# Odd attention: value products in 256-column pairs, grouped by branch

## The chip, the cores and the metric

The kernel runs on one core of a Trainium2 chip, in one launch. The metric is the device time of that core in microseconds, the median of several runs. All matrix products named here are in float32.

## The reference

Two small networks run one after the other on 512 tokens of width 1024. The second one has two layers; the change lies in its second layer, called odd, which is an attention with 16 heads of 64 in four groups that share keys and values, and three branches. Cut to what matters here:

```python
def nsa_attention(q, kc, vc, ks, vs, kw, vw, gate_logit, ...):
    # compressed branch: one key for each stride of 16 tokens (31 of them)
    p_cmp = masked_softmax(q @ k_cmp.T * scale - slopes * distance, cmp_end <= t)
    # selected branch: with 8 blocks and topk = 8 every block is selected
    p_slc = masked_softmax(q @ ks.T * scale - slopes * distance, key <= t)
    # window branch: 512 tokens, here all earlier tokens
    p_win = masked_softmax(q @ kw.T * scale - slopes * distance, key <= t)
    return g0 * (p_cmp @ v_cmp) + g1 * (p_slc @ vs) + g2 * (p_win @ vw)

def odd_layer(x, ...):
    o = nsa_attention(...)
    return x + (o * silu(z)) @ w_out
```

## The kernel before, in words

One instruction stream for each engine is written out by hand, with semaphores between them. The stage that matters is the odd attention: ahead of it stand the projections of the odd layer, behind it the output projection (`oout`, lines 720 to 722 for its products) and the last normalisation.

The 16 heads are taken as eight pairs t = 0..7; both heads of a pair (e = 0, 1) use the same keys and values, those of group g = t // 2. The 512 tokens are four tiles a = 0..3 of 128, and tile a sees the key tiles b = 0..a. Two branches with full keys (`ks`, `vs` and `kw`, `vw`) give ten products of weights by values for each head and branch. They are cut into five parts u, so that each part fills a bank of 512 columns: `ODD_TILES` lists, for each part, (branch, tile a, first column):

- u=0: branch 0, a=3 (one tile of 512 columns)
- u=1: branch 0, a=2 and a=0 (384 and 128)
- u=2: branch 1, a=3
- u=3: branch 1, a=2 and a=0
- u=4: a=1 of branch 0 and of branch 1 (256 and 256)

In the code branch 0 is the selected branch (`ks`, `vs`) and branch 1 the window (`kw`, `vw`). The compressed branch is a part of its own, "blocks", one for each group, so in the list `ODD` it stands in every even pair between u=1 and u=2. `ODD` has 44 parts.

A part n goes through these steps:

1. TensorE, `odd_scores` (L1273; for blocks L1267): scores into one of two PSUM banks PS.
2. VectorE, `odd_x` (L2418): adds the distance table, takes the negative maximum, writes `od_x` (four places). For blocks L2401 to L2410.
3. ScalarE, `odd_exp` (L1737; blocks L1731): exponentials and their sums.
4. VectorE, `odd_invert` (L2440; blocks L2429, L2431): reciprocal of the sums.
5. GpSimd (L2650; blocks L2638, L2641): multiplies by the reciprocal and the gate. It also makes the distance tables (L2629), and low parts of some weights (L2499).
6. TensorE, `odd_transposes` (L1293; blocks L1285): eight 128 x 128 transposes into PC, four for each head. It waits for the copies of the part before.
7. VectorE copies head 0's half of PC (L2457), ScalarE head 1's half (L1754), into `od["PT"]`, which has two places, used in turn; blocks have one copy, by VectorE (L2461).
8. TensorE, `odd_outputs` (L1319): the value products into PD, bank t % 2. The values of one key tile are the stationary operand (64 columns, for head e at partitions 64 e), the transposed weights the moving one, 128 columns each: four products for each head in each part. Blocks have `block_outputs` (L1299, L1302), two products of 512 columns, one for each of the group's two pairs.

After u=4, VectorE multiplies PD by the gate z (L2469, semaphore `ny_raw`), ScalarE copies the result to its rounded part (L1776) and VectorE takes the rest (L2473).

TensorE's order in step n is: transposes of part n, scores of part n+3, outputs of part n-1. VectorE's is: copy of n, `odd_x` of n+3, the reciprocal of n+2, and what follows a pair. ScalarE's is: copy of n, exponentials of n+3, the rounded copy after a pair, and in eight of the steps a piece of the output projection's weights (L1745).

Of the kernel before, what the change touches and what calls it, by code (L numbers as in the profile page):

```python
# [15 lines left out]
ACT = mybir.ActivationFunctionType  # L16
# [3 lines left out]
P = 128  # L20
# [3 lines left out]
S = 512  # L24
# [21 lines left out]
DH = 64  # L46
# [96 lines left out]
for _step in SSD:  # L143
# [5 lines left out]
    if _what in ("B", "C", "x", "z", "s"):  # L149
# [41 lines left out]
ODD = [part for t in range(NH // 2)  # L191
       for part in [("pair", t, 0), ("pair", t, 1)] + ([("blocks", t // 2, 0)] if t % 2 == 0 else []) +
       [("pair", t, u) for u in range(2, 5)]]
# [31 lines left out]
def build(nc, x_in, stream, down, params_in, tables_in, out):  # L225
    ctx = ExitStack()
    with ctx:
# [16 lines left out]
        def sem(name):  # L244
            if name not in sems:
                sems[name] = ctx.enter_context(nc.semaphore(name))
            return sems[name]
# [16 lines left out]
        PC = ctx.enter_context(nc.psum_tensor("PC", [P, 2, BANK], F32))  # L264
        PD = ctx.enter_context(nc.psum_tensor("PD", [P, 2, BANK], F32))
# [5 lines left out]
        def carve(fields):  # L271

            at, views = 0, {}
            for name, *dims in fields:
                n = int(np.prod(dims))
                v = arena[:, at:at + n]
                if len(dims) == 2:
                    v = v.rearrange("p (a b) -> p a b", a=dims[0])
                elif len(dims) == 3:
                    v = v.rearrange("p (a b c) -> p a b c", a=dims[0], b=dims[1])  # L280
                elif len(dims) == 4:
                    v = v.rearrange("p (a b c d) -> p a b c d", a=dims[0], b=dims[1], c=dims[2])
                views[name] = v
                at += n
            assert at <= ARENA, at
            return views
# [129 lines left out]
        def slot_of(stage, r):  # L416
            return nth_plain(stage, r) % R
# [5 lines left out]
        def tile_of(stage, j):  # L423
            return PS[(M0[stage] + j) % 2]
# [96 lines left out]
        def mix_s(n, e):  # L521
            return PS[n % 2][:, e * BANK:(e + 1) * BANK]

        od = carve([("q", 8, S), ("z", 8, S), ("A2", 2, NG, 16, CB + 2), ("ksd", NG, S), ("kwd", NG, S), ("vs", 4, 256), ("vw", 4, 256),
                    ("gates", 48, 4), ("cmp_bias", NH, P), ("h1", 2, P), ("h1v", 2, NG, 4, CB), ("kcmp", P),
                    ("hb", 4), ("mxc", 16), ("rsc", 16), ("cfc", 16), ("cg", NH, 4), ("nm", 4, 4), ("rs", 4, 4),
                    ("gap", 60), ("Vbd", NG, 256), ("PT", 2, 2, S), ("PTc", S)])
# [11 lines left out]
        uT_flat = uT[:, :, :].rearrange("p k l -> p (k l)")  # L539
# [5 lines left out]
        def odd_before(n):  # L545

            pairs = sum(kind == "pair" for kind, _, _ in ODD[:n])
            return pairs, n - pairs

        def odd_tiles(n):  # L550

            return [(b, a, at, P * (a + 1)) for b, a, at in ODD_TILES[ODD[n][2]]]
# [138 lines left out]
        def _(pe):  # L691
            mm = nc.tensor.matmul
# [61 lines left out]
            def project_units(stage, units, moving, high=None, ready=None, within=None):  # L754

                first = units[0] if isinstance(units, range) else 0
                for r in units if isinstance(units, range) else range(units):
                    unit_ready(stage, 0, r)
                    for m in range(2):
                        acquire(pe, stage, 0, 2 * R, 2 * r + m)  # L760
                        new = r == first and m == 0
                        project(stage, 0, 2 * R, 2 * r + m, r, KD, m * P, moving, high, ready if new else None,
                                within if new else None).then_inc(ps_full, 1)
# [450 lines left out]
            for a in range(4):  # L1214
                for k in range(KD):
                    last = mm(tile_of("od_g", 0)[:, a * 48:(a + 1) * 48], h2[:, k, a * P:(a + 1) * P], w_g[:, k, :],
                              start=k == 0, stop=k == KD - 1)
# [8 lines left out]
            for which, stage in enumerate(("ck", "cv")):  # L1226
                for hid in range(2):
                    unit_ready(stage, 0, hid)
                    acquire(pe, stage, 0, 2, hid)
                    t = tile_of(stage, hid)  # L1230
                    w = ring[:, slot_of(stage, hid), :].rearrange("p (k m) -> p k m", k=16)
                    for l2 in range(16):
                        last = mm(t[:, 0:NG * CW].rearrange("p (g c) -> p g c", g=NG), w[:, l2, :],
                                  od["A2"][:, which, :, 2 * l2 % 16, l2 // 8:l2 // 8 + CW], start=l2 == 0, stop=l2 == 15)
# [61 lines left out]
            def block_outputs(g):  # L1296

                pe.wait_ge(sem("cpt_full"), g + 1)
                mm(PD[:, 0, :], od["Vbd"][:, g, 0:P], od["PTc"], start=False, stop=True, skip_group_check=True)  # L1299
                if g:  # L1300
                    pe.wait_ge(sem("ny_raw"), 2 * g)
                mm(PD[:, 1, :], od["Vbd"][:, g, P:2 * P], od["PTc"], start=True, stop=True)  # L1302

            def odd_outputs(n):

                _, t, u = ODD[n]
                f, _ = odd_before(n)
                g = t // 2
                if n == 0:
                    pe.wait_ge(sem("od_full"), 5)  # L1310
                    pe.wait_ge(sem("zs_full"), 16)
                if u == 0 and t % 2 == 0 and t:
                    pe.wait_ge(sem("ny_raw"), t - 1)
                pe.wait_ge(sem("ns_c0"), f + 1)
                pe.wait_ge(sem("ns_c1"), f + 1)
                for branch, a, at, w in odd_tiles(n):
                    for b in range(a + 1):
                        for e in range(2):
                            last = mm(PD[DH * e:DH * e + DH, t % 2, a * P:(a + 1) * P],  # L1319
                                      od["vw" if branch else "vs"][:, b, g * DH:(g + 1) * DH],  # L1320
                                      od["PT"][:, f % 2, e, at + b * P:at + (b + 1) * P],
                                      start=u == 0 and t % 2 == 0 and b == 0, stop=True,
                                      skip_group_check=True)
                if u == 4:
                    last.then_inc(sem("no_full"), 1)

            unit_ready("od_z", 0, 3)
            late_gate(0)
# [9 lines left out]
            for n in range(len(ODD) + 1):  # L1338
                if n < len(ODD):
                    odd_transposes(n)  # L1340
                if n + 3 < len(ODD):
                    odd_scores(n + 3)
                if n and ODD[n - 1][0] == "pair":
                    odd_outputs(n - 1)
                elif n:
                    block_outputs(ODD[n - 1][1])
            project_units("oout", 4, yl, yh, (sem("y_full"), 8))
            stats("last", S)

# [2 lines left out]
        def _(act):  # L1352
            A = nc.scalar.activation
# [315 lines left out]
            for n in range(len(MIX) + 4):  # L1669
                t = n // 7  # L1670
# [28 lines left out]
            for which, stage in enumerate(("ck", "cv")):  # L1699
                for hid in range(2):  # L1700
                    tile_wait(act, stage, 0, 2, hid)
                    t = tile_of(stage, hid)
# [46 lines left out]
            def odd_copy(n):  # L1749
                f, c = odd_before(n)  # L1750
                if ODD[n][0] == "blocks":
                    return
                act.wait_ge(sem("ns_t"), 2 * f + 2)
                A(od["PT"][:, f % 2, 1, :], PC[:, 1, :], ACT.Copy).then_inc(sem("ns_c1"), 1)  # L1754

            for n in range(2):
                odd_exp(n)
# [10 lines left out]
            for n in range(len(ODD) + 3):  # L1768
# [4 lines left out]
                if n >= 3 and ODD[n - 3][0] == "pair" and ODD[n - 3][2] == 4:  # L1773
                    t = ODD[n - 3][1]
# [9 lines left out]
        def _(dve):  # L1784
            V = nc.vector
# [535 lines left out]
            for n in range(len(MIX) + 5):  # L2321
                t = n // 7
# [130 lines left out]
            for n in range(len(ODD) + 4):  # L2453
                if n < len(ODD) and ODD[n][0] == "pair":
                    f, _ = odd_before(n)
                    dve.wait_ge(sem("ns_t"), 2 * f + 1)
                    V.tensor_copy(od["PT"][:, f % 2, 0, :], PC[:, 0, :]).then_inc(sem("ns_c0"), 1)  # L2457
                elif n < len(ODD):
                    _, c = odd_before(n)
                    dve.wait_ge(sem("ct_full"), c + 1)  # L2460
                    V.tensor_copy(od["PTc"], PC[:, 0, :]).then_inc(sem("cpt_full"), 1)  # L2461
                if n + 3 < len(ODD):
                    odd_x(n + 3)
                odd_sum(n + 2)
                odd_invert(n + 2)
                if n >= 2 and n - 2 < len(ODD) and ODD[n - 2][0] == "pair" and ODD[n - 2][2] == 4:
                    t = ODD[n - 2][1]
                    dve.wait_ge(sem("no_full"), t + 1)
                    V.tensor_tensor(sq[:, t % 2, 0:S], PD[:, t % 2, :], od["z"][:, t, :], ALU.mult).then_inc(sem("ny_raw"), 1)  # L2469
                if n >= 4 and n - 4 < len(ODD) and ODD[n - 4][0] == "pair" and ODD[n - 4][2] == 4:  # L2470
                    t = ODD[n - 4][1]
                    dve.wait_ge(sem("ny_high"), t + 1)
                    V.tensor_tensor(r32(yl[:, t, :], 0), sq[:, t % 2, 0:S], split(yh[:, t, :], 0), ALU.subtract  # L2473
                                    ).then_inc(sem("y_full"), 1)
# [318 lines left out]
```

## Time and profile before

| | us |
|---|---|
| median of 3 runs | 2307.72 |
| lowest and highest run | 2302.77, 2310.04 |
| the profiled execution, its own time | 2307.89 |
| span of its profile | 2306.1 |
| odd attention in it, about | 2095.3 to 2248.0 |

The profiler gives each instruction's engine, line, start and duration. A float32 product is run in two passes, so it stands as two instructions (a group of eight value products, four for each head, is x16). The timelines merge neighbouring instructions of one line: the first number is the start, the second the time from the first start to the last end, in square brackets stands the idle time before and what ended it. "issue" is a wait that the profile puts down to no one. Ends of products are modelled, so the distances between starts are the safer measure.

### The profile page before, as it was taken

Reading aid. Unit: us, or ns where it says so; the run is one execution under the profiler, and the core shown is the slowest. Engines: PE = TensorE matmul, PEld = TensorE weight load, DVE = VectorE, ACT = ScalarE, POOL = GpSimd, SP = SyncE. Lnnn points to the kernel's source line nnn. Section 1 sums busy time; section 2 is a strip of 40 time slices with the busy share of each in tenths; the row PEclk is TensorE's granted clock in tenths of the full one; section 3 lists DMA queues with packets and bytes.
Section 4 is the critical chain, followed back from the end, with each engine's and each line's share of the span. In section 5 each row is a group of like instructions: output and inputs, shape, how many; then the busy total and the mean of one; then the engine's idle time right before and its main releaser. Section 6 shows DMA issues by size and latency. Waiting matters only on the chain.

```text
span 2306.1 us, 38488 instructions
## 1 busy us (share of the span) xinstructions
PE 2212.1 (96%) x15924; PEld 1935.8 (84%) x15924; DVE 1240.1 (54%) x1874; ACT 905.4 (39%) x1447; POOL 1006.1 (44%) x924
## 2 busy tenths in 40 slices
PE   8999999889999999999998999999999999999997
PEld 7898988889999999985698989987786577886666
DVE  6776777868527734344369716743214641115763
ACT  4564645533223233346433312333113532126762
POOL 4445444565555540032246555544344234334751
PEclk9999999999999999999999999999999999999999
DMA  4211122122222222220022222222222012350000
GB/s 164 77 72 66 64 74 74 37 74 92 76 99 92 75 100 97 87 74 1 1 92 74 75 102 102 85 77 92 92 92 100 28 56 90 99 179 38 24 15 37
DMA packets 29372, 175.59 MB, mean 76 GB/s; under 512 B 3984, under 2 KB 4496, under 8 KB 12304
## 3 DMA queue, kind: packets, MB, share of 16 engines
q1 hardware_dynamic: 29200, 173.14, 21.3%
q8 instruction: 126, 2.06, 0.4%
q14 instruction: 46, 0.38, 0.0%
HBM read 166.71 MB, written 2.10 MB: 73 GB/s over the span
## 4 chain that ended last, share of the span: by engine, by line
PE 77%; DVE 9%; issue 4%; ACT 3%; POOL 3%; DVEq 2%; SPq 1%; DMA 0%; ACTq 0%; POOLq 0%
PE PS L720 19%; PE PS L721 19%; PE PS L722 19%; POOL ring_r L2490 2%; DVE arena L1933 2%; PE PS L1029 2%; PE PS L1273 2%; PE PC L1293 2%; PE PD L1319 2%; PE PD L720 1%; PE PD L721 1%; PE PD L722 1%; DVE arena L2151 1%; PE PD L1059 1%; DVEq L408 1%
## 5 line engine op out<-in xcount | busy, mean ns | idle before, releaser
L722 PE MATMUL PS<-arena_r,ring_r 128*128 128x264 f32 (+2 forms) x3520 | 1076.9, 306 | 0.0
L2490 POOL TENSOR_TENSOR ring_r<-ring,arena_r 128x512 fp32r<-128x512 f32 (+1 forms) x456 | 596.4, 1338 | 803.6 <-ACT arena_r L1410 803.6
L722 PEld LDWEIGHTS PS<-arena_r,ring_r 128*128 128x128 f32 x3520 | 667.5, 190 | 30.1
L720 PE MATMUL PS<-arena_r,arena_r 128*128 128x264 f32 (+2 forms) x2160 | 654.1, 303 | 17.0 <-POOL arena_r L2508 6.2
L721 PE MATMUL PS<-arena_r,arena_r 128*128 128x264 f32 (+2 forms) x2160 | 647.6, 300 | 0.0
L720 PE MATMUL PS<-arena_r 128*128 128x264 f32 (+3 forms) x1552 | 488.1, 315 | 11.7 <-POOL ring_r L2490 5.1
L1410 ACT ACTIVATE arena_r<-ring 128x2048 fp32r<-128x2048 f32 (+1 forms) x144 | 258.5, 1795 | 499.8 <-PE PS L722 452.6
L720 PEld LDWEIGHTS PS<-arena_r,arena_r 128*128 128x128 f32 x2160 | 409.1, 189 | 41.2 <-issue 9.8
L721 PE MATMUL PS<-uT_r,arena_r 128*128 128x264 f32 (+2 forms) x1360 | 429.9, 316 | 0.0
L721 PEld LDWEIGHTS PS<-arena_r,arena_r 128*128 128x128 f32 x2160 | 409.7, 190 | 13.2 <-issue 0.5
L720 PEld LDWEIGHTS PS<-arena_r 128*128 128x128 f32 x1552 | 295.0, 190 | 33.5 <-POOL ring_r L2490 6.0
L721 PEld LDWEIGHTS PS<-uT_r,arena_r 128*128 128x128 f32 x1360 | 259.2, 191 | 16.8 <-issue 0.5
L2499 POOL TENSOR_TENSOR ring_r<-ring,arena_r 128x512 fp32r<-128x512 f32 x128 | 181.7, 1446 | 160.3 <-ACT arena_r L1410 159.5
L2091 DVE TENSOR_TENSOR hT<-hT,PS 128x512 f32<-128x512 f32 (+2 forms) x56 | 38.8, 693 | 239.7 <-PE PS L722 239.4
L2151 DVE SCALAR_TENSOR_TENSOR arena<-arena,par 128x528 f32<-128x528 f32 (+1 forms) x176 | 158.9, 903 | 13.1
L1539 ACT ACTIVATE arena<-PS 128x528 f32<-128x528 f32 (+1 forms) x76 | 46.0, 605 | 252.3 <-PE PS L722 252.0
L1839 DVE TENSOR_TENSOR arena<-PS,sd 128x512 f32<-128x512 f32 (+1 forms) x46 | 32.0, 697 | 171.6 <-PE PS L722 171.1
L2148 DVE TENSOR_SCALAR arena<-arena,par 128x528 f32<-128x528 f32 (+1 forms) x88 | 79.1, 899 | 67.6 <-ACTq L408 63.6
L2650 POOL TENSOR_SCALAR arena<-arena 128x128 f32<-128x128 f32 (+3 forms) x128 | 78.7, 627 | 68.4 <-DVE arena L2440 68.1
L722 PE MATMUL PD<-arena_r,ring_r 128*128 128x264 f32 (+1 forms) x336 | 97.3, 289 | 0.0
L1933 DVE SCALAR_TENSOR_TENSOR arena<-arena,par 128x528 f32<-128x528 f32 x72 | 79.3, 1101 | 5.9 <-issue 0.5
L1737 ACT ACTIVATE arena<-arena 128x128 f32<-128x128 f32 (+3 forms) x128 | 71.1, 556 | 27.5 <-DVEq L408 22.8
(389 smaller groups left out, 3038.9 us busy)
## 6 DMA issues: line engine op xcount, KB each, us to landing
ring<-stream SPq DMA_DIRECT2D x130, 1024.0 KB, 4.8
ring<-down SPq DMA_DIRECT2D x32, 704.0 KB, 4.0
hT<-x_in SPq DMA_DIRECT2D x4, 528.0 KB, 7.6
arena<-tables SPq DMA_DIRECT2D x4, 512.0 KB, 3.8
arena<-arena SPq DMA_DIRECT2D x16, 128.0 KB, 2.4
out<-uT SPq DMA_DIRECT2D x4, 512.0 KB, 2.8
par<-params SPq DMA_DIRECT2D x1, 1634.5 KB, 14.1
arena<-arena SPq DMA_DIRECT2D x8, 136.0 KB, 3.5
```

Of the source, the lines that this page charges most:

```text
L720: mm(out_, r32(ah), r32(bh), start=start, stop=False)
L721: mm(out_, r32(ah), r32(b), start=False, stop=False)
L722: return mm(out_, r32(a), r32(bh), start=False, stop=stop)
L1029: return mm(sb_z(u, e)[:, a:a + rhs.shape[1]], w, rhs, start=False, stop=True, skip_group_check=True)
L1410: A(r32(high_slot(h)[:, 0:width]), raw_slot(h)[:, 0:width], ACT.Copy).then_inc(sem("high_full"), 1)
L1737: A(x, x, ACT.Exp, bias=od["nm"][:, n % 4, i:i + 1], scale=-1.0, accum_out=od["rs"][:, n % 4, i:i + 1])
L1933: last = V.scalar_tensor_tensor(cv, raw[:, k:k + L], w(k), cv, ALU.mult, ALU.add)
L2148: V.tensor_scalar(out_, ffn[raw][:, 0:width], w(0), b, ALU.mult, ALU.add)
L2151: last = V.scalar_tensor_tensor(out_, ffn[raw][:, k:k + width], w(k), out_, ALU.mult, ALU.add)
L2490: last = G.tensor_tensor(r32(low[:, cut]), raw[:, cut], split(high[:, cut]), ALU.subtract)
L2499: last = G.tensor_tensor(r32(low[:, cut]), raw[:, cut], split(high[:, cut]), ALU.subtract)
L2650: last = G.tensor_scalar(x, x, od["rs"][:, n % 4, i:i + 1], od["gates"][:, 6 * t + 3 * e + 1 + b, a:a + 1], ALU.mult, ALU.mult)
```

## The change

The value products are put in another order and in wider pieces. After the transposes of u=0 and u=1 nothing is multiplied; their copies go to two places of a branch, and the products of the branch follow later: in the step of u=2 those of key tiles 0 and 1, in the step of u=3 those of key tiles 2 and 3. The products of branch 1 (parts u=2 and u=3) all stand in the step of u=4. Part u=4 itself is multiplied in the step after it, as before (`odd_second`). Where a key tile b has weights for both tiles 2 and 3, the two are the moving operand of one product, 256 columns from two places (`pair[:, :, e, ...]`), into 256 neighbouring columns of PD. There are four places for weights: two of branch 0 in `od["PT"]`, two of branch 1 in the second half of uT. `block_outputs` now begins both banks of PD (start=True), with its wait on `ny_raw` written for each, and all products of the two other branches add to what stands there.

```diff
+        def odd_weights(branch):
+            return od["PT"] if branch == 0 else uT_flat[:, 4 * S:8 * S].rearrange("p (n e c) -> p n e c", n=2, e=2)
+        def odd_slot(n):
+            u = ODD[n][2]
+            return odd_weights(u in (2, 3))[:, int(u in (0, 2)), :, :]
...
             def block_outputs(g):
                 pe.wait_ge(sem("cpt_full"), g + 1)
-                mm(PD[:, 0, :], od["Vbd"][:, g, 0:P], od["PTc"], start=False, stop=True, skip_group_check=True)
-                if g:
-                    pe.wait_ge(sem("ny_raw"), 2 * g)
-                mm(PD[:, 1, :], od["Vbd"][:, g, P:2 * P], od["PTc"], start=True, stop=True)
-
-            def odd_outputs(n):
+                for half in range(2):
+                    if 2 * g + half > 1:
+                        pe.wait_ge(sem("ny_raw"), 2 * g + half - 1)
+                    elif half == 0:
+                        pe.wait_ge(sem("od_full"), 5)
+                        pe.wait_ge(sem("zs_full"), 16)
+                    mm(PD[:, half, :], od["Vbd"][:, g, half * P:(half + 1) * P], od["PTc"], start=True, stop=True)
+
+            def odd_values(t, e, branch, b, a, weights):
+                n = weights.free_size() // P
+                return mm(PD[DH * e:DH * e + DH, t % 2, a * P:(a + n) * P], od["vw" if branch else "vs"][:, b, t // 2 * DH:(t // 2 + 1) * DH],
+                          weights, start=False, stop=True, skip_group_check=True)
+
+            def odd_branch(n, blocks):
                 _, t, u = ODD[n]
+                branch = u // 2
                 f, _ = odd_before(n)
-                g = t // 2
-                if n == 0:
-                    pe.wait_ge(sem("od_full"), 5)
-                    pe.wait_ge(sem("zs_full"), 16)
-                if u == 0 and t % 2 == 0 and t:
-                    pe.wait_ge(sem("ny_raw"), t - 1)
+                pe.wait_ge(sem("ns_c0"), f + 1)
+                pe.wait_ge(sem("ns_c1"), f + 1)
+                pair = odd_weights(branch)
+                for b in blocks:
+                    for e in range(2):
+                        if b < 3:
+                            odd_values(t, e, branch, b, 2, pair[:, :, e, b * P:(b + 1) * P])
+                        else:
+                            odd_values(t, e, branch, b, 3, pair[:, 1, e, b * P:(b + 1) * P])
+                    if b == 0:
+                        for e in range(2):
+                            odd_values(t, e, branch, 0, 0, pair[:, 0, e, 3 * P:4 * P])
+
+            def odd_second(n):
+                _, t, _ = ODD[n]
+                f, _ = odd_before(n)
                 pe.wait_ge(sem("ns_c0"), f + 1)
                 pe.wait_ge(sem("ns_c1"), f + 1)
                 for branch, a, at, w in odd_tiles(n):
-                    for b in range(a + 1):
+                    for b in range(2):
                         for e in range(2):
-                            last = mm(PD[DH * e:DH * e + DH, t % 2, a * P:(a + 1) * P],
-                                      od["vw" if branch else "vs"][:, b, g * DH:(g + 1) * DH],
-                                      od["PT"][:, f % 2, e, at + b * P:at + (b + 1) * P],
-                                      start=u == 0 and t % 2 == 0 and b == 0, stop=True,
-                                      skip_group_check=True)
-                if u == 4:
-                    last.then_inc(sem("no_full"), 1)
+                            last = odd_values(t, e, branch, b, a, odd_slot(n)[:, e, at + b * P:at + (b + 1) * P])
+                last.then_inc(sem("no_full"), 1)
+
+            def odd_outputs(n):
+                kind, t, u = ODD[n - 1]
+                if kind == "blocks":
+                    block_outputs(t)
+                elif u == 4:
+                    odd_second(n - 1)
+                if n < len(ODD):
+                    kind, t, u = ODD[n]
+                    if kind == "pair" and u in (2, 3):
+                        odd_branch(n - u + 1 - (t % 2 == 0), range(2) if u == 2 else range(2, 4))
+                    elif kind == "pair" and u == 4:
+                        odd_branch(n - 1, range(4))
...
-                if n and ODD[n - 1][0] == "pair":
-                    odd_outputs(n - 1)
-                elif n:
-                    block_outputs(ODD[n - 1][1])
+                if n:
+                    odd_outputs(n)
...
-                A(od["PT"][:, f % 2, 1, :], PC[:, 1, :], ACT.Copy).then_inc(sem("ns_c1"), 1)
+                A(odd_slot(n)[:, 1, :], PC[:, 1, :], ACT.Copy).then_inc(sem("ns_c1"), 1)
...
-                    V.tensor_copy(od["PT"][:, f % 2, 0, :], PC[:, 0, :]).then_inc(sem("ns_c0"), 1)
+                    V.tensor_copy(odd_slot(n)[:, 0, :], PC[:, 0, :]).then_inc(sem("ns_c0"), 1)
```

## Rows read from the trace of the kernel before

**Rows 1.** The page, part 1: busy time and share of the span, instructions.

```profile
PE 2212.1 (96%) x15924; PEld 1935.8 (84%) x15924; DVE 1240.1 (54%) x1874; ACT 905.4 (39%) x1447; POOL 1006.1 (44%) x924
```

**Rows 2.** Stages: window, length, busy of PE, PEld, DVE, ACT, POOL; granted clock; DMA.

```profile
2095.30:2248.00 152.70, 140.94 (x1338) 100.60 (x1337) 109.21 (x362) 110.78 (x308) 99.52 (x151) 0.99 0.05 15
2133.10:2136.50 3.40, 3.40 (x27) 3.02 (x26) 2.42 (x5) 1.39 (x3) 1.35 (x3) 0.50 0.00 0
```

**Rows 3.** Timeline of TensorE, pair t=5 from u=0, then pair t=6.

```profile
2195.16 1.06 PE L1293 MATMUL PC<-par,arena 128*128 128x128 f32 x8 [0.53 <-issue]
...
2197.22 1.09 PE L1319 MATMUL PD<-arena 128*64 128x128 f32 x16
...
2199.27 1.14 PE L1273 MATMUL PS<-arena 64*128 64x256 f32 x8
...
2201.95 1.06 PE L1293 MATMUL PC<-par,arena 128*128 128x128 f32 x8 [0.53 <-issue]
2202.95 1.13 PE L1273 MATMUL PS<-arena 64*128 64x512 f32 x4
...
2208.54 1.07 PE L1293 MATMUL PC<-par,arena 128*128 128x128 f32 x8 [0.32 <-issue]
2209.54 1.98 PE L1267 MATMUL PS<-arena 64*128 64x32 f32 x32
...
2212.47 1.09 PE L1293 MATMUL PC<-par,arena 128*128 128x128 f32 x8
2213.49 1.13 PE L1273 MATMUL PS<-arena 64*128 64x512 f32 x4
...
2217.86 1.09 PE L1319 MATMUL PD<-arena 128*64 128x128 f32 x16
2218.89 0.66 PE L1285 MATMUL PC<-par,arena 128*128 128x128 f32 x4
2219.47 1.14 PE L1273 MATMUL PS<-arena 64*128 64x256 f32 x8
...
2232.74 1.06 PE L1293 MATMUL PC<-par,arena 128*128 128x128 f32 x8 [0.53 <-issue]
```

**Rows 4.** Timelines of VectorE (first row) and ScalarE, same pair t=5.

```profile
2197.34 0.56 DVE L2418 CUSTOM_DVE_ANT_0 arena<-PS,uT 128x384 f32<-128x384 f32 x1 [0.82 <-PE PS L1273]
...
2198.87 0.61 ACT L1737 ACTIVATE arena<-arena 128x384 f32<-128x384 f32 x1 [1.41 <-DVEq L408]
...
2201.26 0.60 ACT L1754 ACTIVATE arena<-PC 128x512 f32<-128x512 f32 x1
...
2207.33 0.63 ACT L1776 ACTIVATE arena_r<-sq 128x512 fp32r<-128x512 f32 x1
2207.87 0.58 ACT L1754 ACTIVATE arena<-PC 128x512 f32<-128x512 f32 x1
```

**Rows 5.** Timeline of TensorE, the stage's end: two groups of value products together.

```profile
2245.69 1.97 PE L1319 MATMUL PD<-arena 128*64 128x128 f32 x32
2247.59 0.50 PE L720 MATMUL PS<-arena_r,arena_r 128*128 128x512 f32 x1
```

**Rows 6.** Timelines of GpSimd and VectorE, the blocks of pair t=6.

```profile
2217.55 1.05 POOL L2641 TENSOR_TENSOR arena<-arena 128x512 f32<-128x512 f32 x1
...
2220.23 0.68 DVE L2461 COPY arena<-PC 128x512 f32<-128x512 f32 x1
```

**Rows 7.** The chain that ended last, pair t=6: start, length, what.

```profile
2223.72 1.05 PE PD L1299 x2
...
2225.63 0.32 issue
```

**Rows 8.** Timeline of TensorE around the drop of the clock, end of pair t=1.

```profile
2130.27 1.07 PE L1293 MATMUL PC<-par,arena 128*128 128x128 f32 x8 [0.84 <-issue]
...
2133.18 1.97 PE L1319 MATMUL PD<-arena 128*64 128x128 f32 x16
2135.09 1.76 PE L1293 MATMUL PC<-par,arena 128*128 128x128 f32 x8
```

## The prediction

> **What bounds the kernel now.** I read the page's first part first: TensorE is busy for 96% of the span [rows 1], so a change matters only through TensorE's time or through its waits. Next the table by stages: the odd attention takes about 152.7 us, and TensorE is busy for 140.94 of them [rows 2]. So about 12 us of waiting are open in this stage. In the timeline of TensorE I then looked at what precedes each start. A step n is three groups: the transposes of part n, the scores of part n+3, the value products of part n-1. From one start to the next the transposes take 1.00 to 1.02 us, the scores 1.06 (both together 2.06, from 2195.16 to 2197.22), the products 1.03 (2217.86 to 2218.89), so a full step is 3.1 us; some steps have 0.3 to 0.5 us of idle time before their transposes [rows 3].
>
> That idle time has one cause. ScalarE copies part n's second half out of PSUM, then does the exponentials of part n+3, then copies part n+1; TensorE may not transpose part n+2 before this last copy. In an odd pair: the scores end, the product group behind them starts at 2197.22; VectorE takes the scores from 2197.34, ScalarE's exponentials run from 2198.87, its copy from 2201.26 for 0.60, the transposes start at 2201.95 [rows 3, 4]. So from E, the end of the score group, to the transposes two steps on, the **chain** is 4.73 us. TensorE's own way over the same distance (products, transposes, scores, products) is 1.03 + 2.07 + 1.03 = 4.13, which is why it idles. For parts of one 512-column tile the chain is shorter: from E = 2202.95 + 1.06 = 2204.01 to 2208.54 it is 4.53, and of this 0.54 is the copy L1776 that stands between (2207.33 to 2207.87) [rows 3, 4]; 3.99 without it.
>
> **The change, part by part.**
>
> *Wider products.* The columns that stream stay the same: of a branch, tile a=3 has four products, a=2 three and a=0 one; three of these eight now go along with another, so five products of 256, 256, 256, 128 and 128 columns have the same 1024. What a wider product saves is shown by the scores: four instructions of 512 columns take 1.13 us, eight of 256 columns 1.14 [rows 3]. Columns set the time, the number of instructions does not. I take 0 to 0.01 us per branch, at most 0.2 us for 16 branches, and count it as nothing.
>
> The Trainium skill, TensorE: Matmul & The Clock Gate, Back-to-back issue gap, speaks otherwise: in streams of weight load and matmul it has about 81 ns per matmul at 128 columns and 131 at 512, so that four times the columns cost only 1.6 times as much. An estimate by that page would put a 256-column product near 98 ns where two narrow ones take 162. The trace doesn't agree: 1.13 against 1.14 us at equal columns. What the rule would do here is the second rival below.
>
> *Moved products.* A unit is one 128-column product for both heads, four instructions in the trace. Two value groups back to back, 32 instructions, take 2247.59 - 2245.69 = 1.90 us, one of 16 takes 1.03 [rows 3, 5]; so a unit costs 0.2175 us and a group 0.16 us beside. Before, each step has four units: 1.03. After, in the order of the steps: u=0 four (the second part, as before), u=1 none, blocks none, u=2 five (1.25), u=3 three (0.81), u=4 eight (1.90). A pair has 20 units as before, and one or two groups fewer.
>
> *Waits.* The two copies that a branch waits for are those that the step's own transposes have waited for already; nothing new is queued behind them. The block products keep their place, and their second half waits for the same reading of PD. The four weight places add no wait: each is overwritten by a copy behind a transpose that TensorE issues after the last product that reads it. The copies keep their size and engine, no DMA moves, nothing on SP or GpSimd changes.
>
> *An odd pair, both kernels*, T = start of the transposes, 0 at u=0, E = T + 2.07:
> - u=1: 2.07 + 1.03 = 3.10 in both.
> - u=2: before TensorE would be ready at 6.20, after at 5.17; the chain from E = 2.07 ends at 6.80 in both. The time won is idle.
> - u=3: before 6.80 + 3.10 = 9.90; after 6.80 + 2.07 + 1.25 = 10.12.
> - u=4: TensorE 13.00 in both, chain 6.80 + 2.07 + 4.53 = 13.40 in both.
> - next u=0, past the block scores, which take 1.90 instead of 1.06 (2209.54 to 2212.47, less 1.03): before 13.40 + 1.00 + 1.90 + 1.03 = 17.33 (the trace has 2212.47 - 2195.16 = 17.31), after 13.40 + 2.90 + 1.90 = **18.20**. That is **+0.87**.
>
> So units are taken from a step that waits for ScalarE in any case and given to one, u=4, where TensorE is last.
>
> *An even pair, after*, 0 at u=0. u=1: 3.10. Blocks: TensorE 5.17, but GpSimd's product L2641 ends 2217.55 + 1.05 - 2214.55 = 4.05 after E (2213.49 + 1.06), with 0.15 to react 6.27 (before 6.42). u=2: TensorE 7.91; VectorE's copy L2461 ends at 2220.91, 3.05 after E of u=1 (2217.86), with 0.1 to react 3.10 + 2.07 + 3.15 = 8.32 (before 2219.47 + 1.07 + 1.03 - 2212.47 = 9.10, since TensorE still had a group there). u=3: 8.32 + 2.07 + 1.91 for the block products (2223.72 to 2225.63) + 1.25 = 13.55 (before 13.48, of which the last 0.32 was a wait). u=4: + 2.88 = 16.43. Next u=0: + 2.07 + 1.90 = **20.40**, against 2232.74 - 2212.47 = 20.27 before: **+0.13** [rows 3, 6, 7]. Here 0.78 us are won up to u=2 and lost again in u=2 and u=4.
>
> *Sum.* Four odd pairs at 0.87 and about three and a half even ones at 0.13: 3.5 + 0.5 = **+4 us**. The last pair has no block scores, but its eight units at u=4 stand on the way to the output projection just so. Bounds: ScalarE's extra weight pieces in eight steps already lengthen the waits there (0.84 us at 2130.27 [rows 8]) and can hide some of it: +2.5. If VectorE or GpSimd meet the bunched scores less well, each even pair may lose the 0.78 again: 4 + 3.5 x 0.78 = +6.7. The profiled execution is 2307.89, 0.17 above the median of 2307.72: 2307.9 + 4 = **2311.9**, 2312 as a median.
>
> **The rivals.**
> 1. *The clock drops more often* (slower). In the stage the granted clock fell once, 2133.1 to 2136.5, to 0.50, the lower level of 1.2 GHz; ahead of it TensorE had idled 0.84 us and run the 32-column block scores [rows 2, 8]. A value group took 1.97 instead of 1.09 us there, the transposes behind it 1.76 instead of 1.09: a drop costs about 1.5, at most half of 3.4. In the changed kernel the idle time before u=2 of each odd pair grows from 0.53 to 1.63 us, and at the blocks of each even one there are 1.5 us in two waits. Seven such places, all followed by a stretch in which TensorE is last. Against it: the other two block scores, after 0.32 us of idle time, kept the clock. Two more drops give 2311.9 + 3 = 2315, past the bound of 0.3%; three 2316.5; all seven 2322.
> 2. *Wide products are cheap.* If one of 256 columns cost no more than one of 128, a branch would have five units: u=2 three (0.81), u=3 two (0.60), u=4 five (1.25). The odd pair becomes 9.90, 13.40, 13.40 + 2.90 + 1.25 = 17.55: still +0.22, since the chain holds u=2 to u=4. In the even pair u=3 came 2225.95 - 2220.54 = 5.41 us after E of the blocks' step (2219.47 + 1.07), by ScalarE; so now not before 7.91 + 5.41 = 13.32, and the next u=0 not before 13.32 + 2.07 + 4.73 = 20.12, 0.15 less than 20.27. Together about +0.5: 2308. Even this limit gives no gain that can be seen.
> 3. *The wait absorbs it.* If eight units at u=4 are covered by something the rows don't show as last, the saved groups remain: some ten of 0.16 us, -1.6: 2306.
> 4. *It does not do what it says*: if products of two weight places were split again, the order alone would act: the forecast's own time.
>
> **How the numbers follow.** Forecast (2309 to 2314.5, the fourth rival in it) 0.64; more clock drops, enough to pass the bound, 0.20 (2315 to 2322); cheap wide products 0.04 and absorbed 0.07 (both 2305 to 2309); something outside of these 0.05, split 0.03 faster, 0.02 slower. A measurement of this kernel can tell 0.3%, about 6.9 us, from no change. Faster 0.03; slower 0.20 + 0.02 = 0.22; within 0.75. The runs shown scatter from 2302.77 to 2310.04, which the range must take in: 2306 to 2319.
>
> **What would show it.** Right: in odd pairs the transposes of u=2 follow 1.6 us of idle time and their distance from u=0 is still 6.8 us; the u=4 group takes 1.9 us and the next u=0 comes 0.9 us later than before; the span from blocks to blocks grows by about 1 us; eight products' worth of columns costs the same. Wrong: if the exponentials start earlier and the 6.8 us shrink, if a group of five 256- and 128-column products is clearly under 1.9 us, or if the granted clock in the stage shows several drops.

## The result and the profile after

The changed kernel takes 2312.43 us (median of 22 runs) against 2307.63 (22 runs): 1.0017 times as long, 95% interval 1.0009 to 1.0024, so slower by 2.1 to 5.5 us, less than the 0.3% that were to count as a change. The forecast was 2312, from 2307.9 + 4. Two runs with more than twice the time, one of each kernel, are left out of the ratio.

The page's first part: TensorE has 192 instructions less and is busy as long as before [rows 1].

```profile
span 2310.8 us, 38099 instructions
PE 2211.0 (96%) x15732; PEld 1927.9 (83%) x15732; DVE 1239.3 (54%) x1874; ACT 905.1 (39%) x1447; POOL 1006.1 (44%) x924
```

TensorE's timeline of the same odd pair t=5 as in [rows 3], from u=0, and the even pair t=6 behind it (start, length, line, operands, instructions, idle time before). Transposes are now line 1302, scores 1282, block scores 1276, value products 1319, block products 1314:

```profile
2197.02 1.09 PE L1302 MATMUL PC<-par,arena 128*128 128x128 f32 x8
...
2200.14 1.09 PE L1302 MATMUL PC<-par,arena 128*128 128x128 f32 x8
2201.16 1.13 PE L1282 MATMUL PS<-arena 64*128 64x256 f32 x8
2203.84 1.07 PE L1302 MATMUL PC<-par,arena 128*128 128x128 f32 x8 [1.55 <-issue]
...
2207.13 1.09 PE L1302 MATMUL PC<-par,arena 128*128 128x128 f32 x8
...
2210.44 1.06 PE L1302 MATMUL PC<-par,arena 128*128 128x128 f32 x8 [0.34 <-issue]
...
2213.34 1.95 PE L1319 MATMUL PD<-uT,arena 128*64 128x256 f32 x20
2215.22 1.09 PE L1302 MATMUL PC<-par,arena 128*128 128x128 f32 x8
...
2218.33 1.09 PE L1302 MATMUL PC<-par,arena 128*128 128x128 f32 x8
2219.35 1.14 PE L1282 MATMUL PS<-arena 64*128 64x384 f32 x8
2221.50 0.63 PE L1294 MATMUL PC<-par,arena 128*128 128x128 f32 x4 [1.01 <-POOL arena L2678]
...
2223.72 1.06 PE L1302 MATMUL PC<-par,arena 128*128 128x128 f32 x8 [0.53 <-DVE arena L2498]
...
2228.92 1.09 PE L1302 MATMUL PC<-par,arena 128*128 128x128 f32 x8
...
2235.78 1.09 PE L1302 MATMUL PC<-par,arena 128*128 128x128 f32 x8
```

What is to be seen: behind u=1 TensorE now idles 1.55 us, where it had idled 0.53; u=2 starts 6.82 us after u=0 as it did before (6.79). The eight units at u=4 take 2215.22 - 2213.34 = 1.88 us. From u=0 to the next u=0 it is 18.20 us instead of 17.31, in the even pair 20.56 instead of 20.27.

ScalarE's timeline of the same odd pair shows why u=2 doesn't come sooner. The exponentials (line 1774) start where VectorE has read the scores, at 2200.76, 1.65 us after the end of the scores (2199.11, the start of the group behind them); the copy (1791) stands behind them, as in [rows 4], and u=2 starts at 2203.84, 0.09 us after its end:

```profile
2200.76 0.62 ACT L1774 ACTIVATE arena<-arena 128x384 f32<-128x384 f32 x1 [1.56 <-DVEq L408]
...
2203.15 0.60 ACT L1791 ACTIVATE arena<-PC 128x512 f32<-128x512 f32 x1
```

Over the whole stage, from the first transposes to the output projection, the two profiles differ by 154.70 - 152.22 = 2.5 us. That the kernel before lost time to the one drop of the clock [rows 8] hides some of it: the experiment with the four places below has the order of the kernel before and no drop in the pairs t=1 and t=2, which there take 17.82 and 21.38 us instead of 18.72 and 21.86, so the drop cost 1.4 us. Without it the stage is 3.9 us longer. The stages table of the changed kernel shows no drop in the stage (window, length, busy of PE, PEld, DVE, ACT, POOL, granted clock, DMA), but one far ahead of it, where the kernel before had the full clock; the spans differ by 4.7 us.

```profile
79.60:83.00 3.40, 3.40 (x17) 3.40 (x17) 2.21 (x4) 1.73 (x5) 1.08 (x1) 0.50 0.31 77
2096.60:2251.30 154.70, 137.44 (x1143) 91.18 (x1141) 108.76 (x361) 110.53 (x308) 99.26 (x151) 1.00 0.04 15
```

### The profile page after: what moved, and what is told of

Read it like the earlier page. It is cut to its first block, busy times and chain, and to the rows that moved or that the text cites. A ratio compares the mean times of both kernels' runs of the same rounds, so it can differ in the third digit from the quotient of the medians.

```text
span 2310.8 us, 38099 instructions
## 1 busy us (share of the span) xinstructions
PE 2211.0 (96%) x15732; PEld 1927.9 (83%) x15732; DVE 1239.3 (54%) x1874; ACT 905.1 (39%) x1447; POOL 1006.1 (44%) x924
## 4 chain that ended last, share of the span: by engine, by line
PE 76%; DVE 10%; issue 4%; ACT 3%; POOL 3%; DVEq 2%; SPq 1%; DMA 0%; ACTq 0%; POOLq 0%
PE PS L729 19%; PE PS L730 19%; PE PS L731 18%; POOL ring_r L2527 2%; DVE arena L1970 2%; PE PS L1038 2%; PE PC L1302 2%; PE PD L1319 2%; PE PS L1282 2%; PE PD L729 1%; PE PD L730 1%; PE PD L731 1%; DVE arena L2188 1%; PE PD L1068 1%; DVEq L408 1%
```

## The experiments

The theory (A): TensorE's way through a pair is bounded in some steps by ScalarE, whose copy stands behind its exponentials, and in the others by TensorE's own work; the change takes products from a step of the first kind and adds them to one of the second; their width does nothing. The rivals, besides a price or a gain of the width itself: all of TensorE's work counts wherever it stands (B), or none of it does (C); the waits have another source than the copy's place (D); with the waits gone the two orders are level (E); the four weight places cost something (F). Each experiment changes one thing of it. The table has the medians, the ratio to runs of the kernel before that were taken beside each (their medians are 2307.77 us for the first four experiments, 2308.50 for the next three and 2308.36 for the last) and, from each profile, the two distances that the recurrence of the prediction gave: the odd pair t=5 and the even pair t=6, from u=0 to the next u=0. The last column is the distance from u=0 of pair t=1 to the first product of the output projection, in the same profiles. Only two of them have a drop of the clock there, the kernel before (1.4 us, so 129.9 without it) and e1_narrow (at the end of t=1, a pair that takes 20.34 us there and 18.71 in the changed kernel, so 133.0 without it). This column is the sharpest measure: it leaves out what scatters in the rest of the kernel, while most of the intervals of the medians overlap.

| kernel | median us | ratio to before, 95% interval | odd pair t=5 | even pair t=6 | t=1 to the end |
|---|---|---|---|---|---|
| before | 2307.63 | 1 | 17.31 | 20.27 | 131.23 |
| after | 2312.43 | 1.0017 (1.0009 to 1.0024) | 18.20 | 20.56 | 132.89 |
| e1_narrow | 2312.68 | 1.0018 (1.0007 to 1.0028) | 18.22 | 20.59 | 134.67 |
| e2_work_u1 | 2310.21 | 1.0007 (0.9993 to 1.0020) | 18.20 | 20.56 | 132.94 |
| e3_work_u4 | 2316.38 | 1.0036 (1.0021 to 1.0052) | 19.50 | 20.56 | 138.13 |
| e4_spread | 2308.90 | 1.0005 (0.9992 to 1.0017) | 17.52 | 20.53 | 131.42 |
| e5_split_before | 2301.10 | 0.9960 (0.9945 to 0.9975) | 16.40 | 19.16 | 123.19 |
| e6_split_after | 2310.85 | 1.0012 (1.0001 to 1.0023) | 16.66 | 20.57 | 128.99 |
| e7_split_spread | 2305.38 | 0.9981 (0.9970 to 0.9992) | 16.37 | 19.94 | 126.49 |
| e8_places | 2309.38 | 1.0003 (0.9991 to 1.0015) | 17.31 | 20.28 | 129.87 |

### Order alone: the wide products split again

```diff
-                        if b < 3:
-                            odd_values(t, e, branch, b, 2, pair[:, :, e, b * P:(b + 1) * P])
-                        else:
-                            odd_values(t, e, branch, b, 3, pair[:, 1, e, b * P:(b + 1) * P])
+                        if b < 3:
+                            odd_values(t, e, branch, b, 2, pair[:, 0, e, b * P:(b + 1) * P])
+                    for e in range(2):
+                        odd_values(t, e, branch, b, 3, pair[:, 1, e, b * P:(b + 1) * P])
```

> The changed kernel with its order and its four weight places, but each 256-column product split into two of 128 columns again. Theory A (the order of the products costs the time, their width nothing): 2312.5 us, within 1 us of the changed kernel; eight products' worth of a branch still takes 1.9 us. Rival W (the width, or the operand from two places, has a price or a gain of its own): if the wide products cost the 4.8 us, this one comes back to about 2308; if they give something, it is slower than 2314.

Measured 2312.68 us. The group at u=4 in TensorE's timeline is now 32 instructions instead of 20 and takes 2220.87 - 2218.97 = 1.90 us, against 1.88:

```profile
2218.97 1.97 PE L1319 MATMUL PD<-uT,arena 128*64 128x128 f32 x32
2220.87 1.09 PE L1302 MATMUL PC<-par,arena 128*128 128x128 f32 x8
```

So twelve instructions less are worth 0.02 us per branch, 0.3 us in all, and the kernel's loss stays when the width is taken back. The rival of a price or a gain by the width falls.

### The same extra work in two places

Twelve products that nothing uses, once in the step that waits, once in the step where TensorE should be last:

```diff
+            def fill(n, units):
+                pe.wait_ge(sem("ns_x"), min(n + 3, len(ODD)))
+                for k in range(units):
+                    for e in range(2):
+                        mm(odd_s(n + 4, e)[DH * e:DH * e + DH, 0:P], od["vs"][:, k % 4, 0:DH],
+                           od["PT"][:, 1, e, k % 4 * P:(k % 4 + 1) * P], start=True, stop=True)
...
+                    if kind == "pair" and u == 1 and t % 2:      # u == 4 in the second kernel
+                        fill(n, 6)
```

> The changed kernel with twelve more value products (six units, 1.47 us with the group's fixed part) after the scores in the step of u=1 of each odd pair; their result goes to a free score bank and is used by nothing. Theory A (this step waits for ScalarE in any case, 1.55 us idle behind it): 5.9 us of TensorE work for 0 to 0.6 us, 2312.5 to 2313. Rival B (TensorE is last everywhere, so all its work counts): 2318.

> The same twelve products behind the eight units in the step of u=4 of each odd pair instead. Theory A (there TensorE is last): 4 x 1.3 = 5.2 us more, 2317.6. Rival B: the same as with the products at u=1. Rival C (what counts is only how much work TensorE has, and much of it is covered anywhere): both 2312.5.

Measured 2310.21 and 2316.38 us. TensorE's timelines, first with the work (line 1357) at u=1, from u=0 to u=2 and the next u=0:

```profile
2199.75 1.09 PE L1302 MATMUL PC<-par,arena 128*128 128x128 f32 x8
...
2204.95 1.53 PE L1357 MATMUL PS<-arena 128*64 128x128 f32 x24
2206.57 1.07 PE L1302 MATMUL PC<-par,arena 128*128 128x128 f32 x8
...
2217.95 1.09 PE L1302 MATMUL PC<-par,arena 128*128 128x128 f32 x8
```

and with it at u=4, from u=0:

```profile
2202.56 1.09 PE L1302 MATMUL PC<-par,arena 128*128 128x128 f32 x8
...
2218.87 1.95 PE L1319 MATMUL PD<-uT,arena 128*64 128x256 f32 x20
2220.65 1.48 PE L1357 MATMUL PS<-arena 128*64 128x128 f32 x24
2222.06 1.09 PE L1302 MATMUL PC<-par,arena 128*128 128x128 f32 x8
```

At u=1 the 1.5 us of work vanish in the wait: u=2 still comes 6.82 us after u=0, the next u=0 18.20 us after it. At u=4 the same work adds 19.50 - 18.20 = 1.30 us, 5.2 in four pairs as expected. From t=1 to the end the rows have 132.94 - 132.89 = 0.05 us for the work at u=1 and 138.13 - 132.89 = 5.24 for the same work at u=4. In the medians it is -2.2 and 4.0 us, and there the intervals overlap with that of the changed kernel, so it is the rows that tell the two apart. Rivals B (all work counts) and C (none does) fall.

### Key tiles 2 and 3 of branch 1 to the next u=1

```diff
-                        odd_branch(n - 1, range(4))
+                        odd_branch(n - 1, range(2))
+                    elif kind == "pair" and u == 1 and t:
+                        odd_branch(n - 3, range(2, 4), True)
+                else:
+                    odd_branch(n - 2, range(2, 4), True)
```

The semaphore that tells VectorE that a pair is ready goes along, behind the last of these products.

> The changed kernel, but of branch 1 only the key tiles 0 and 1 (five units) stand in the step of u=4; the key tiles 2 and 3 (three units) go to the step of u=1 of the next pair, and the pair is told ready after them. Theory A: the pile at u=4 falls from 1.90 to 1.25 us and the step that waits takes 0.81 more: by the recurrence an odd pair takes 17.55 instead of 18.20 us and an even one 20.35 instead of 20.40, so 2312.4 - 2.8 = 2309.6. Rival W: the width is unchanged, so 2312.4.

Measured 2308.90 us, odd pair 17.52 (expected 17.55), even pair 20.53 (20.35). The wait behind u=1 is shorter by the work that came, the group at u=4 by the work that left:

```profile
2197.87 0.87 PE L1319 MATMUL PD<-uT,arena 128*64 128x256 f32 x8
2199.49 1.06 PE L1302 MATMUL PC<-par,arena 128*128 128x128 f32 x8 [0.75 <-issue]
...
2208.98 1.30 PE L1319 MATMUL PD<-uT,arena 128*64 128x256 f32 x12
```

The medians differ by 3.5 us (expected: 2.8), with intervals that overlap; from t=1 to the end the rows have 132.89 - 131.42 = 1.5 us. The odd pairs t=1, t=3 and t=5 each gain 0.66 to 0.68, the last pair nothing, and the even pair t=4 loses 0.60 (21.16 instead of 20.56), with TensorE waiting for GpSimd's multiplication in it. The gain is about half of what was expected, but it comes with every width as in the changed kernel: the order is what costs.

### The copy between the halves of the exponentials

If the theory holds, the waits must go when ScalarE's copy no longer stands behind all the exponentials. ScalarE's loop, in the kernel before, in the changed one and in the spread one:

```diff
-            def odd_exp(n):
+            def odd_exp(n, heads=range(2)):
...
-                for e in range(2):
+                for e in heads:
...
+            odd_copy(0)
             for n in range(len(ODD) + 3):
-                if n < len(ODD):
-                    odd_copy(n)
                 if n + 3 < len(ODD):
-                    odd_exp(n + 3)
+                    odd_exp(n + 3, [0])
+                if n + 1 < len(ODD):
+                    odd_copy(n + 1)
+                if n + 3 < len(ODD):
+                    odd_exp(n + 3, [1])
```

> The kernel before, with one thing changed on ScalarE: the exponentials of part n+3 are cut between the heads, and the copy of part n+1 stands between the two halves instead of behind both. Theory A (TensorE's waits come from this copy standing behind the exponentials): from the end of the scores to the transposes two steps on it is now 0.12 + 1.47 + 0.06 + 1.15 + 0.1 + 0.6 + 0.1 = 3.6 us instead of 4.73, less than TensorE's own 4.13, so the waits go: an odd pair takes 16.3 instead of 17.31 us, an even one 19.4 instead of 20.27; 2307.7 - 7 = 2301, up to 2304 if GpSimd's products become last at times. Rival D (the waits come from something else, such as the scores' bank or GpSimd): no change, 2307.7.

> The changed kernel with the same cut on ScalarE. Theory A: the transposes of u=2 in an odd pair come 5.7 instead of 6.8 us after those of u=0, the pile at u=4 stays: an odd pair 16.7 instead of 18.20 us, an even one 20.4; 2312.4 - 6 = 2306.5, so faster than the changed kernel, and still slower than the kernel before with the same cut by some 5 us. Rival D: no change, 2312.4. Rival E (without the wait the new order is as good as the old one): level with the kernel before with the cut.

> The changed kernel with the cut on ScalarE and branch 1's key tiles 2 and 3 in the next step of u=1. Theory A: an odd pair 16.3, an even one 19.8, so close to the kernel before with the cut: 2302 to 2303. Rival E: level with the changed kernel with the cut alone.

Measured 2301.10, 2310.85 and 2305.38 us. The kernel before with the cut is the fastest of all, faster than both kernels of this case. Its timeline of TensorE, u=0 to the next u=0 of pair t=5, has no idle time at all (compare [rows 3]):

```profile
2191.70 1.09 PE L1293 MATMUL PC<-par,arena 128*128 128x128 f32 x8
...
2197.92 1.09 PE L1293 MATMUL PC<-par,arena 128*128 128x128 f32 x8
...
2204.14 1.09 PE L1293 MATMUL PC<-par,arena 128*128 128x128 f32 x8
...
2208.10 1.09 PE L1293 MATMUL PC<-par,arena 128*128 128x128 f32 x8
```

u=2 comes 6.22 us after u=0 instead of 6.79, the odd pair takes 16.40, as do t=1 and t=3. From t=1 to the end it is 123.19 us instead of 129.9, 6.7 less (expected: 7). Not every wait goes: the even pair t=4, where GpSimd also makes weight pieces, takes 20.60 (the pairs t=2 and t=6 19.16), with waits of 1.02 and 0.35 us for GpSimd's multiplication. Rival D (the waits come from something else) falls for the waits behind the copy.

The changed kernel with the cut has the odd pair at 16.66, as expected, and the even one at 20.57, as expected not better than without the cut: its waits there are GpSimd's product and VectorE's copy, which the cut doesn't touch. But its time is 4.4 us above what I expected, and only 1.6 us under the changed kernel, within the two intervals. In the pairs t=3 and t=4, where GpSimd also makes weight pieces, the profile has 17.15 and 21.45 us (18.17 and 20.56 without the cut), and TensorE waits for GpSimd's multiplications there, in t=4 for that of u=1 (line 2692) and of the blocks (2683):

```profile
2172.82 0.63 PE L1302 MATMUL PC<-par,arena 128*128 128x128 f32 x4 [0.28 <-POOL arena L2692]
2173.80 0.66 PE L1302 MATMUL PC<-par,arena 128*128 128x128 f32 x4 [0.35 <-POOL arena L2692]
2176.49 0.63 PE L1294 MATMUL PC<-par,arena 128*128 128x128 f32 x4 [0.97 <-POOL arena L2683]
```

So of the 6 us the rows from t=1 to the end gave 132.89 - 128.99 = 3.9. That the medians show only 1.6 of them may be scatter: the 11 runs had a mean granted clock of 0.988, those of the changed kernel 0.989, and 0.001 goes with 1.4 to 1.7 us (last section). With the wait gone, the new order is still slower than the old one with the same cut: by 9.7 us in the medians, with intervals that lie apart, and by 128.99 - 123.19 = 5.8 in the rows (expected: some 5). So rival E (level) falls too. With the spread order the odd pair is even with the old order (16.37), the even pair is not (19.94 against 19.16), and the time is 2 to 3 us over what was expected.

### The four weight places alone

```diff
-                                      od["PT"][:, f % 2, e, at + b * P:at + (b + 1) * P],
+                                      odd_slot(n)[:, e, at + b * P:at + (b + 1) * P],
...
-                A(od["PT"][:, f % 2, 1, :], PC[:, 1, :], ACT.Copy).then_inc(sem("ns_c1"), 1)
+                A(odd_slot(n)[:, 1, :], PC[:, 1, :], ACT.Copy).then_inc(sem("ns_c1"), 1)
...
-                    V.tensor_copy(od["PT"][:, f % 2, 0, :], PC[:, 0, :]).then_inc(sem("ns_c0"), 1)
+                    V.tensor_copy(odd_slot(n)[:, 0, :], PC[:, 0, :]).then_inc(sem("ns_c0"), 1)
```

> The kernel before with nothing but the four weight places: the copies of u=2 and u=3 go to the second half of uT and are read from there, products, order and widths as before. Theory A (only the order costs): an odd pair still 17.3 us, an even one 20.3 to 20.9, 2307.7 to 2308.5. Rival F (the places cost: copies into uT, where the distance tables lie too, or reads from it are slower): a part of the 4.8 us, so 2309 to 2312, with longer copies in the rows.

Measured 2309.38 us, interval 0.9991 to 1.0015. The median alone lies in the range of rival F (2309 to 2312) and can't decide; the rows can. The pairs take 17.31 and 20.28 us as before, and from t=1 to the end it is 129.87 against 129.9 of the kernel before without its drop. The groups by line of this kernel, 2200 to 2245 (count, then busy time and mean ns), show VectorE's copies into uT and into the arena:

```profile
L2466 DVE COPY arena<-PC 128x512 f32<-128x512 f32 x7 | 4.7, 670 | 1.0 <-PE PC L1302 1.0
L2466 DVE COPY uT<-PC 128x512 f32<-128x512 f32 x6 | 4.1, 683 | 1.8 <-PE PC L1302 1.8
```

683 against 670 ns, where the same copies of the kernel before, all into the arena, have a mean of 675; the places cost nothing that shows. Rival F (the places cost something) falls.

## Why the prediction was right, point by point

- *Wider products save nothing.* Right: 1.88 us with 20 instructions, 1.90 with 32. The estimate by the Trainium skill's figures (TensorE: Matmul & The Clock Gate, Back-to-back issue gap), which had a 256-column product near 0.6 of two narrow ones, doesn't hold for these float32 products.
- *The prices of the groups.* 1.25, 0.81 and 1.90 us were worked out from one group of 16 and one of 32; measured from start to start are 2207.13 - 2205.90 = 1.23, 0.80 (in the even pair t=6, where no wait follows) and 1.88. The timelines have one group less in a pair (five before, four after), not one or two.
- *The odd pair.* Forecast 3.10, 6.80, 10.12, 13.40, 18.20 us; the trace has 3.12, 6.82, 10.11, 13.42, 18.20. The idle time behind u=1 was forecast at 1.63 and is 1.55.
- *The even pair.* Forecast 3.10, 6.27, 8.32, 13.55, 20.40; the trace has 3.11, 6.28, 8.50, 13.70, 20.56. The term that was too small is in u=2, and it is not VectorE's copy: the scores of u=1 end at 2219.35 + 1.06 = 2220.41 and the copy (line 2498) at 2223.46, 3.05 us later, as the forecast had read from the kernel before. It is the 0.1 us to react: the transposes start at 2223.72, 0.26 after the copy, and just so in the pairs t=2 and t=4. Behind ScalarE's copy it is 0.09, behind GpSimd's product of the blocks (2220.31 + 1.05 to 2221.50) 0.14; why VectorE's takes longer is not shown. The rows of GpSimd and of VectorE in the changed kernel:

```profile
2220.31 1.05 POOL L2678 TENSOR_TENSOR arena<-arena 128x512 f32<-128x512 f32 x1
...
2222.78 0.68 DVE L2498 COPY arena<-PC 128x512 f32<-128x512 f32 x1
```

- *What an even pair loses.* In the forecast an even pair lost 0.13 us, in the last one it lost 0.29. In the two earlier even pairs it gained 0.67 and 0.35 (21.86 and 20.91 before, 21.19 and 20.56 after), the first with 0.5 of the clock's drop in it; the forecast had taken all alike. From blocks to blocks, t=4 to t=6, it is 38.76 us instead of 37.56, where about 1 us more was to be seen.
- *The sum.* +4 us was forecast from four odd and three and a half even pairs. In the profiles it is 2.5, and 3.9 with the drop of the clock taken out; the medians have 4.8, the interval 2.1 to 5.5. The pairs do not share it as forecast: the first steps up to t=1, where TensorE now waits 0.51 and 0.61 us for GpSimd, and the last pair took 0.8 and 0.65 us more, the odd pairs t=3 and t=5 0.86 and 0.89. With the drop taken out, the four odd pairs lost 3.3 (forecast: 3.5). The even ones lost 0.57 together (forecast: 0.5), but as 0.82, -0.19, -0.35 and 0.29: that their sum came out is luck.
- *The rivals.* More drops of the clock: the profile after has none in the stage, in spite of the longer idle times. Of the eight experiments' profiles six have one in the first 15 us of the stage, in kernels of either order, and e1_narrow a second one at the end of pair t=1, at 2139, the place of the drop in the kernel before. The price of a drop, forecast at 1.5 us, was 1.4 and 1.6 (20.34 - 18.71). Cheap wide products and work that is absorbed: the split products and the extra work at u=4 speak against both. Two sums in these rivals are rough: four odd pairs at 0.22 and three and a half even ones at -0.15 make 0.4 and not 0.5, and the saved groups are eight of 0.16 us, 1.3 and not 1.6.
- *The one cause of the idle time.* That it is the copy behind the exponentials was argued in the prediction. The cut shows it for the waits behind that copy: they go when it is moved, and the odd pairs then take what TensorE's own work takes. For all the idle time it was said too widely: in t=4 TensorE waits for GpSimd's multiplication, 0.22 and 0.35 us in the kernel before and 1.02 and 0.35 us with the cut.

## What to carry to other kernels

Where two engines take turns at being last within a loop, an operation is free in one step and dear in another: find for each step which wait ends last, and move work towards the steps that wait, not away from them. Before work is moved around a wait, look at the queue of the engine that ends it: here one copy between two halves of the exponentials was worth 6.5 us, more than any order of the products. Fewer and wider matmuls did nothing for these float32 products, whose time went with the columns and not with the instructions; two score groups of equal columns and unlike width in the same trace told that beforehand.

## What the runs showed of the hardware

The granted clock falls to 0.50, the lower level of 1.2 GHz, in places of which some change from profile to profile. The drop at 79.60 in the changed kernel came 0.6 us behind an idle time of 0.78 us, in an otherwise busy stretch:

```profile
78.97 0.36 PE L729 MATMUL PD<-arena_r 128*128 128x264 f32 x1 [0.78 <-DVE arena L2043]
...
79.74 0.42 PE L731 MATMUL PD<-arena_r,ring_r 128*128 128x264 f32 x1
```

In the kernel before, TensorE was just as busy in the 9.6 us ahead of that point (8.82 us, 68 instructions in both; the first row is the changed kernel's) and kept 1.00, though the same idle time of 0.78 us stands before the same product there, at 79.39:

```profile
70.00:79.60 9.60, 8.82 (x68) 7.61 (x67) 8.39 (x18) 5.43 (x5) 3.89 (x4) 1.00 0.12 48
...
70.00:79.60 9.60, 8.82 (x68) 7.60 (x67) 8.32 (x17) 5.41 (x5) 3.48 (x3) 1.00 0.16 67
79.60:83.00 3.40, 3.40 (x30) 3.40 (x29) 2.63 (x5) 1.34 (x6) 1.49 (x2) 1.00 0.13 29
```

The drops go with the scatter between runs of one kernel: a straight line through the times and mean granted clocks of the 21 runs of the changed kernel gives 1.4 us for each 0.001 of clock (and carries two thirds of their variance), one through 35 runs of the kernel before 1.7; on these lines, at a clock of 0.989, the two take 2312.37 and 2308.62 us, 3.75 us apart, near the 3.9 of the rows of the stage. The idle time of 1.55 us behind u=1, three times that of before, stands in the profiles of the changed kernel, of e1_narrow and of e3_work_u4, and brought no drop in any of their odd pairs from t=3 on.
